# Quarter pieces in the levels of a triangular inverse, one block for both passes, and a reordered VectorE queue in a pooling + RWKV-7 layer

## The reference

```python
mod = silu(c) @ w_ada + b_ada;  shift, scale, gate = split(mod, 3)
u = rms_norm(x, norm_gain) * (1 + scale) + shift
proj = u @ w_in                                   # 1024 -> pool v|g, then r|k|v|w_down|a_down|gate
y_pool = multiscale_pool(proj[pool v]) * silu(proj[pool g])
# RWKV-7, per head of 64, state S of 64 x 64:
#   S_t = S_{t-1} diag(w_t) + (S_{t-1} a_t) b_t^T + v_t k_t^T ;  y_t = S_t r_t
y_rwkv = group_norm(y) * lnx_w + lnx_b + (sum r*k*r_k) * v, times silu(gate)
h = x + gate * (concat(y_pool, y_rwkv) @ w_out)
return rms_norm(h, final_gain)
```

## Time and profile before

| | us |
|---|---|
| median of 3 runs | 2912.44 |
| time of the profiled execution | 2913.32 |
| its span, first to last instruction | 2911.6 |
| PE busy | 2801.9 |
| DVE busy | 1560.3 |
| ACT busy | 1096.5 |
| POOL busy | 477.5 |

### The profile page before, as it was taken

One profiled execution on the slowest core, in us unless ns is written; L12 is line 12 of the kernel. 1 busy time (PEld: TensorE's weight loads), 2 busy tenths in 40 slices (PEclk: granted clock), 3 DMA queues, 4 the chain that ended last, 5 costly groups with the idle time before them and its releaser, 6 DMA issues.

```text
span 2911.6 us, 75522 instructions
## 1 busy us (share of the span) xinstructions
PE 2801.9 (96%) x30981; PEld 2327.5 (80%) x30981; DVE 1560.3 (54%) x3137; ACT 1096.5 (38%) x2531; POOL 477.5 (16%) x627
## 2 busy tenths in 40 slices
PE   7999999999799999999999999999999999999996
PEld 6777777777588888888888888888888888888884
DVE  2421121121366666666666666666666666666664
ACT  3333333232133333344433333344443343344442
POOL 3201101101111211111111211111111211111210
PEclk8999999999899999999999999999999999999997
DMA  8622322322100000010000000000000000001000
GB/s 340 238 74 99 115 87 93 108 99 67 66 9 23 24 23 23 24 38 24 28 26 23 23 24 23 23 31 31 24 30 24 23 24 23 24 26 35 23 16 23
DMA packets 68707, 153.09 MB, mean 53 GB/s; under 512 B 3977, under 2 KB 37342, under 8 KB 66398
## 3 DMA queue, kind: packets, MB, share of 16 engines
q1 hardware_dynamic: 63134, 130.08, 12.9%
q0 software_dynamic: 1680, 11.01, 0.9%
q10 hardware_dynamic: 3632, 7.87, 0.7%
HBM read 98.61 MB, written 50.33 MB: 51 GB/s over the span
## 4 chain that ended last, share of the span: by engine, by line
PE 52%; DVE 11%; ACT 6%; issue 5%; DVEq 0%; DMA 0%; ACTq 0%
PE bank L928 26%; PE bank L977 12%; PE bank L964 8%; PE bank L1096 2%; DVE SV L1455 2%; DVE LA L1480 1%; ACT sig L1167 1%; ACT sig L1166 1%; DVE mix L1371 1%; PE bank L938 1%; DVE t L1400 1%; ACT UV L1257 1%; DVE LA L1476 1%; DVE kk L1407 1%; DVE t L1408 1%
## 5 line engine op out<-in xcount | busy, mean ns | idle before, releaser
L928 PE MATMUL bank<-xT,w 128*128 128x128 f32 x8704 | 1106.6, 281 | 7.4 <-DMA xT<-xt_dram 7.4
L928 PEld LDWEIGHTS bank<-xT,w 128*128 128x128 f32 x8704 | 1011.9, 192 | 43.5 <-issue 8.5
L1199 ACT ACTIVATE XX<-bank 128x256 f32<-128x256 f32 x320 | 123.0, 384 | 910.3 <-PE bank L977 897.9
L347 PE MATMUL bank<-xT,w 128*128 128x256 f32 x2048 | 448.6, 381 | 4.8 <-ACT xT L467 4.8
L347 PEld LDWEIGHTS bank<-xT,w 128*128 128x128 f32 x2048 | 391.6, 191 | 65.4 <-issue 10.5
L1465 DVE TENSOR_TENSOR XV<-bank,level_mask 128x256 f32<-128x256 f32 x320 | 132.9, 423 | 327.4 <-PE bank L977 318.1
L964 PE MATMUL bank<-wo,Y 128*128 128x512 f32 x512 | 233.5, 600 | 4.6 <-DVE Y L1425 4.6
L379 PE MATMUL bank<-wo,yc 128*128 128x512 f32 x512 | 226.5, 596 | 4.5 <-DVE yc L698 4.5
L977 PEld LDWEIGHTS bank<-XX,AI 64*64 64x64 f32 x5120 | 163.6, 136 | 63.5 <-issue 52.0
L671 DVE TENSOR_SCALAR gate<-gate 128x1024 f32<-128x1024 f32 x16 | 11.1, 694 | 368.0 <-ACT gate L487 368.0
L977 PE MATMUL bank<-XX,AI 64*64 64x64 f32 x5120 | 185.8, 222 | 4.6 <-DVE XX L1498 4.6
(11 more groups left out here) (182 smaller groups left out, 3588.2 us busy)
## 6 DMA issues: line engine op xcount, KB each, us to landing
x_in<-in_x SPq DMA_DIRECT2D x16, 1024.0 KB, 7.5
xr<-in_x SPq DMA_DIRECT2D x32, 512.0 KB, 4.4
xt_dram<-xT SPq DMA_DIRECT2D x32, 512.0 KB, 8.6
h_dram<-xr SPq DMA_DIRECT2D x32, 512.0 KB, 2.6
xT<-xt_dram SPq DMA_DIRECT2D x32, 512.0 KB, 3.3
gate_row<-h_dram SPq DMA_DIRECT2D x32, 512.0 KB, 3.3
out<-gate_row SPq DMA_DIRECT2D x32, 512.0 KB, 2.6
w<-in_w_in POOLq DMA_DIRECT2D x8, 1088.0 KB, 11.0
```

Of the source, the lines that this page charges most:

```text
L347: last = nc.tensor.matmul(bank[t // 2][:, (t % 2) * T1:(t % 2 + 1) * T1], w1[:, k, t * P:(t + 1) * P], xT[:, k, :], start=(k == 0), stop=( ...
L928: last = nc.tensor.matmul(bank[b][:, q * P:(q + 1) * P], w2[:, k, (t0 + q) * P:(t0 + q + 1) * P], xT[par][:, k, :], start=(k == 0), stop=( ...
L1199: s(nc.scalar.activation(XX[j][:, k].rearrange(flat), bank[2 + j][:, 256 * k:256 * (k + 1)], ACT.Copy), xx_ready, hold=False)
```

## The change

1. `inverses` works in four pieces for each product of a level: chunk j and a, a pair of the four head pairs. Each piece has a PSUM bank of its own (2, 3, 5, 6), `lx` in its columns 0 to 127 and `xx` in 128 to 255, and its own waits and signals. VectorE's masks and ScalarE's copies are of 128x128 in place of 128x256 elements. The fill behind `xx` is moved in front of it (3 half slots in place of 2 and 1), `other` stands there too, and so `lx` of the next level follows `xx` directly. The last level keeps 2 and 1.
2. On VectorE `new_state(1)` is split. The sum stays. The multiplication with the decay moves behind the LA writes of the next block. `shift(n+1, 3)` moves ahead of `replaced_key`. TensorE no longer waits for the state at the block's start, but for the sum ahead of the Gram products and for the state ahead of `from_state(0)`.
3. Both passes are in one block. The prologue of pass 2 stands ahead of the last `project_out` pair on TensorE; VectorE does those residuals within its prologue; SP issues the first `xT` loads before it stores the last h. Tiles are ordered anew so that a tile of pass 2 overlaps one of pass 1 that is done, with waits for that on PE, POOL, ACT and DVE.

The diff, without the re-indentation and cut to its core:

```diff
             def inverses(fill, other):
-                def heads(o, lhsT, rhs):
-                    for p in range(NP):
+                def heads(o, lhsT, rhs, a):
+                    for p in (2 * a, 2 * a + 1):
                         for e in range(2):
                             h = half(e)
-                            last = nc.tensor.matmul(o[h, p * HD:(p + 1) * HD], lhsT[h, p], rhs(h, p), start=True, stop=True)
+                            c = (p - 2 * a) * HD
+                            last = nc.tensor.matmul(o[h, c:c + HD], lhsT(h, p), rhs(h, p), start=True, stop=True)
                 for i in range(LV):
-                    for j in range(NC):
+                    for j, a in PIECES:
                         if i:
-                            s.wait(xx_ready, NC * (i - 1) + j + 1)
+                            s.wait(xx_ready, piece(i - 1, j, a))
                         else:
                             s.wait(x1_ready, j + 1)
                         let_through(pe, pe_gate)
-                        heads(bank[5 + j][:, 0:256], AI[j], lambda h, p: XX[j][h, 0, p]).then_inc(lx_ps.sem, 1)
-                    fill(2)
-                    for j in range(NC):
-                        s.wait(xv_ready, NC * i + j + 1)
+                        heads(level_bank(j, a)[:, 0:128], lambda h, p: AI[j][h, p], lambda h, p: XX[j][h, 0, p], a)\
+                            .then_inc(lx_ps.sem, 1)
+                    fill(3 if i < LV - 1 else 2)
+                    if i in (2, 3):
+                        other(i - 2)
+                    for j, a in PIECES:
+                        s.wait(xv_ready, piece(i, j, a))
                         if i:
                             s.wait(xt_ready, NC * (i - 1) + j + 1)
                         let_through(pe, pe_gate)
...
-                    fill()
-                    if i in (2, 3):
-                        other(i - 2)
+                fill()
+                s.wait(xx_ready, piece(LV - 1, 1, 1))
...
             def take_inverse(i):
-                for j in range(NC):
-                    s.wait(xx_ps, NC * i + j + 1)
-                    s(nc.scalar.activation(XX[j][:, k].rearrange(flat), bank[2 + j][:, 256 * k:256 * (k + 1)], ACT.Copy),
+                for j, a in PIECES:
+                    s.wait(xx_ps, piece(i, j, a))
+                    s(nc.scalar.activation(XX[j][:, k, 2 * a:2 * a + 2].rearrange(flat), level_bank(j, a)[:, 128:256], ACT.Copy),
                       xx_ready, hold=False)
...
             def level(i):
-                if i:
-                    for j in range(NC):
-                        s.wait(xx_ready, NC * (i - 1) + j + 1)
+                for j in range(NC):
+                    if i:
+                        s.wait(xx_ready, piece(i - 1, j, 1))
                         s(nc.vector.transpose(XX[j][:, 1].rearrange(flat), XX[j][:, 0].rearrange(flat)), xt_ready, hold=False)
-                for j in range(NC):
-                    s.wait(lx_ps, NC * i + j + 1)
-                    s(nc.vector.tensor_tensor(XV[j][:, :, :], per_head(bank[5 + j][:, 0:256]), ...
+                    for a in range(2):
+                        s.wait(lx_ps, piece(i, j, a))
+                        s(nc.vector.tensor_tensor(XV[j][:, 2 * a:2 * a + 2, :], per_head(level_bank(j, a)[:, 0:128]), ...
...
             # TensorE, run(n)
-                pv.wait(s_ready, NC)              # ahead of bonus_sum
+                pv.wait(sum_ready, 1)             # ahead of the Gram products
+                pe.wait_ge(h_ready1.sem, h_ready1.at(N1 - 1, 4))   # first block, ahead of the BK transposes
+                pv.wait(carried_ready, 1)         # in from_state(0)
...
             # VectorE, run(n): behind the LA writes
+                if not first:
+                    new_state(NC - 1, pv, carried_ready)      # the two L1455 multiplications of block n-1
                 s(nc.vector.tensor_copy(dend[:, :, :].unsqueeze(3), chunks(sig[:, 0])[:, :, :, C - 1:C]), hold=False)
...
             # VectorE, end of run(n)
-                new_state(1)
+                state_sum(1)                                  # the two L1452 additions
                 if ahead:
-                    replaced_key()
                     shift(n + 1, 3)
+                    replaced_key()
...
             # between the passes
+            # SP: after the last step of pass 1
+                sp.wait_ge(xT_stored, 32 * N1)
+                sp.wait_ge(proj_ps.sem, proj_ps.at(N1 - 1, 4))
+                first_loads()
                 store(N1 - 1)
+            # TensorE: run(N1 - 1), then meanwhile()
+                pe.wait_ge(w2_loaded, 16 * (KT + 1))
+                pe.wait_ge(u_ready1.sem, u_ready1.at(N1 - 1, PT))
+                for m in range(len(SLOTS)):
+                    project(m, 0, 0, prologue=True)
+                pe.wait_ge(gate_ready1.sem, gate_ready1.at(N1 - 1, 2))
+                low_rank()
+                key_norm()
                 for j in range(2):
                     project_out(N1 - 1, j)
+            # VectorE: after mixed(N1 - 1)
+                shift(0, 0); tanh(); shift(0, 1); [wo2 *= gate_row]; shift(0, 2); key(); shift(0, 3); clamp(0); clamp(1)
+                first_residual(N1 - 1, 0)
                 decay_sum(); new_key(); replaced_key()
+                first_residual(N1 - 1, 1)
```

More of the change, by code:

```diff
@@ L1012, in from_state @@
                         for p in range(NP):
                             for e in range(2):
[L1014 to L1022 removed]
+                                o = j * 256 + p * HD
@@ new lines, in run @@
+                                last = nc.tensor.matmul(bank[5][half(1 - e), o:o + HD], mix[:, 8 + p, j * C:(j + 1) * C],
+                                                        center[:, half(e)], start=True, stop=True)
+                    last.then_inc(vt_ps.sem, 1)
+                    s.wait(kt_ready, 1)
+                    s.wait(bk_ready, 1)
+                    s.wait(rg_ready, 1)
+                    if first:
+                        pe.wait_ge(h_ready1.sem, h_ready1.at(N1 - 1, 4))
+                    else:
+                        pv.wait(rs_ready, 1)
@@ L1037, in state_and_output @@
+                    last.then_inc(bt_ps.sem, 1)
+                    s.wait(lhs_ready, 1)
+                    if not first:
+                        pv.wait(sum_ready, 1)
+                    for j in range(NC):
                         for p in range(NP):
                             for e in range(2):
-                                last = nc.tensor.matmul(bank[7][half(e), p * HD:(p + 1) * HD], BT[e][:, j, p], UV[e][:, p],
-                                                        start=True, stop=True)
@@ L1041, in state_and_output @@
-                        last.then_inc(s_ps.sem, 1)
-                        if j:
-                            s.wait(y_ready, j)
-                        for p in range(NP):
-                            for e in range(2):
-                                o = bank[6][half(e), p * HD:(p + 1) * HD]
-                                nc.tensor.matmul(o, UV[e][:, p], SM[j][e][:, p, 1], start=True, stop=False)
-                                last = nc.tensor.matmul(o, SV[e][:, p], LA[e][:, p, j, 1], start=False, stop=True)
@@ new lines, in run @@
+                                last = nc.tensor.matmul(bank[((2, 3), (4, 7))[j][e]][:, p * P:(p + 1) * P], BK[half(e), p, j].rearrange(flat),
+                                                        LA[e][half(e), p, j].rearrange(flat), start=True, stop=True)
+                                if p == NP - 1:
+                                    last.then_inc(gram_ps.sem, 1)
+                    fill(6)
+                    s.wait(bt_ready, 2)
+                    inverses(fill, (lambda h: None) if first else out_half)
@@ new lines, in run @@
+                    from_state(0, first)
+                    if ahead:
+                        low_rank()
+                    solve(0)
+                    fill(2)
+                    state_and_output(0, first)
+                    fill(2)
+                    if ahead:
+                        key_norm()
+                    from_state(1)
+                    fill(1)
+                    solve(1)
+                    fill(2)
+                    state_and_output(1)
+                    fill(len(SLOTS))
@@ new lines, in run @@
+                    if not first:
+                        group_scale(1 - par)
+                    level(0)
+                    if not first:
+                        group_gate()
+                    if ahead:
+                        shift(n + 1, 0)
+                    level(1)
+                    if ahead:
+                        tanh()
+                    level(2)
+                    s.wait(erg_ready, 1)
+                    s(nc.vector.tensor_scalar(rgate[:, :, :], rgate[:, :, :], LN_MAX, None, ALU.min), gclamp_ready)
@@ new lines, in run @@
+                    level(3)
+                    if not first:
```

(26 more changed lines are left out.)

1939 lines of the change are left out of this document (957 added, 982 removed).

## The result

The changed kernel takes 2815.86 us (median of 4 runs, 2815.16 to 2816.39) against 2912.61 for the kernel before, a ratio of 0.9667 with a 95% interval of 0.9653 to 0.9682. The forecast was 2845 us with a range of 2822 to 2876. The direction was right, and the gain of 97 us was over 40% larger than the 67.5 forecast, outside the range.

What follows compares the result with a forecast made beforehand. TensorE's queue was taken to bound the kernel. Gains of 24 us (levels), 30 (block's end) and 13.5 (between the passes) summed to 67.5 us off the median 2912.4: 2845 us, range 2822 to 2876.

Steps and rivals of the forecast that it cites:

- What bounds it: In the 31 intervals between blocks, TensorE's queue sets the end at 65.4 us each, at granted clock 1.00.
- The block's end: Moving the shift and state multiplication removes 1.12 us of waits less 0.15 a block: 30 us, bounds 10 and 35.
- new waits: At the block's end, 0.2 us taken by nearness to the sums, spread as 0.15 us a block.
- The levels: Moved fills in the inverse's levels gain net 0.78 us a block, 24 us in 31 blocks, bounds 0 to 40.
- round trips: Between small and full tiles on TensorE, 0.32 us each; four gone a block, 1.28 us.
- The 0.12 us charged to each handoff: From xx to the next lx, assumed cost of TensorE's doubled waits, 0.5 us a block; bounds 0 and 0.32 each.
- zero margin: At xx to next lx, the first copy lets lx start at 0.96 us, just when PE arrives.
- GpSimd: At the block's end, the shift passes beside GpSimd's BK unslowed and kk waits 0.2 us; otherwise kk loses 1.0.
- Between the passes: Lacing pass 2's prologue with the last out projection brings block 0's first level forward 13.5 us, bounds 9 and 16.
- The last block: It has no fill and changes by some 2 us either way.
- The rivals: Handoffs eat round trips 2869 us (0.14); VectorE bounds block's start 2865 (0.12); slower 2941 (0.05); no change 2912 (0.03).
- The emptying of PSUM: In the levels, the handoffs rival: split copies, each awaiting its signal, remove the 24 us, giving 2869 us; chance 0.14.

Runs made afterwards that it cites:

- no_order: Kernel after with VectorE's old order at the block's end and TensorE's old wait for the state ahead of bonus_sum: 2870.9 us, ratio 0.9852.
- late_state: Kernel after with the state multiplication back at the block's end behind replaced_key, the shift staying moved: 2842.3 us, ratio 0.9759.
- chunks: Kernel after with whole chunks as pieces, two per product, copies and masks of 128x256: 2849.1 us, ratio 0.9782.
- shift_between: Kernel after with shift 3 moved between the two halves of BK on VectorE: 2842.3 us, ratio 0.9759.
- hold_gone: shift_between with GpSimd's BK product of later blocks cut to 4 of 64 columns, leaving out computation: 2815.4 us, ratio 0.9664.
- lace_only: Kernel after with the old end order and old fill places; quarter pieces and lacing stay: 2904.2 us, ratio 0.9971.

## Why the prediction was wrong

The mechanisms were the right ones. Two terms of the sum were mis-sized, both the same way: the block's end and the handoffs in the levels.

- **What bounds it** was right: TensorE's queue, at a granted clock of 1.00 inside the loop both times.
- **The block's end: the step that failed.** I sized it by the idle times, 1.12 us a block, less 0.15 of new waits: 30 us. The steps gave 1.62 a block, 50 us, and the undo 51 by its intervals, 55 by its time. (Even the idle was misread: 1.7 of the 8.3 us for LA stood in block 0, ahead of the 31 intervals, so what was printed came to 1.07 a block.) The prediction had said that a busy PE can lose time in its steps, read the levels by starts, and then read the block's end by the idle times. A late signal cost 0.15 to 0.17 us in its own step beyond the idle shown and up to 0.10 in the next one (`no_order`, `late_state`), and 0.28 with none shown in `chunks`. The 0.17 is the stretch by which neighbouring groups of matmuls overlap when the signal is in time. The new waits did not come: LA ended 0.45 us before the Gram products began (1674.09 to 1674.54).
- **The levels.** Four round trips of 0.32 us: from the first lx to `from_state(0)` it was 33.08 us (1729.03 to 1762.11) and is 31.83 (1682.03 to 1713.86), so 1.25 against 1.28. The price was right. The 0.12 us charged to each handoff was wrong, with nothing measured behind it: 24 us forecast, 39 found. What I took for zero margin had 0.09 more, since the copy took 0.28 and not 0.37. The quarter pieces are needed all the same, as `chunks` shows at 0.28 a handoff.
- **GpSimd.** That the shift would pass beside GpSimd's product and the multiplication would not was right. I had not seen that this is nearly half of the reorder's worth, 0.73 of 1.66 us a block: an operation with two SBUF inputs behind the sums meets the hold (`shift_between`, `hold_gone`).
- **Between the passes.** 13.5 us forecast, 9.5 found in the two traces. PE started the projection at 740.93 in place of 737.3, and 2.9 of those 3.6 us are a first pass that ended 2.9 later in that execution (730.97). The stretch itself, from there to block 0's first level, went from 88.07 to 75.66 us, 12.4 less. The waits that I had counted as removed are in part still there: PE waits 3.3 us for `xr` and 2.0 for LA. The slow clock shrank with the idle time, from 0.66 over 25.4 us to 0.81 over 18.0.
- **The last block** gave 3.2 us where I had 2 either way. That is no gain of the change: the kernel after took 71.2 us there the second time, 2.6 more than the kernel before.
- **The rivals** fell. The emptying of PSUM did not become the bound: four copies of 128x128 took 0.98 us beside 0.98 of matmuls. The section "PSUM Bottleneck" of the Trainium skill's page "TensorEngine Tiling (Array Packing)", which I had weighed for one of them, says that it may; this trace does not show it, and copies twice as wide lost 33 us (`chunks`). VectorE was at 66% in the loop and in time at each place.

The terms against the traces: 50 + 39 - 4.3 + 9.5 + 3.2 = 97. The 4.3 are the first two intervals. In the kernel before they took 65.78 and 65.20 us, so they gained 1.5 us, and not twice the 2.87 of the levels and the block's end:

```profile
788.62:853.84 65.22, 58.97 (x862) 54.91 (x861) 41.43 (x94) 24.73 (x69) 14.31 (x16) 0.95 0.07 26
853.84:918.13 64.29, 63.10 (x877) 55.14 (x876) 41.36 (x101) 27.70 (x76) 11.57 (x13) 1.00 0.08 27
```

Part of that is the slow clock, 0.95 in the first one, and part two gaps of 1.0 and 1.2 us in the middle of `from_state`, with no wait behind them. What they are stays open.

## What to carry to other kernels

On a pipelined engine, price a wait by the step from start to start against the same step undisturbed, not by the idle time shown: here the idle times named 32 of 85 us, and in `chunks` the waits named 0.5 of 33. Before you compare two totals to a few microseconds, look for a stretch that no edit touches, and see how much it varies. Group work by the array's tile shape, since each round trip cost 0.31 us here, and cut what follows it into pieces just small enough that the first copy is back when the last piece leaves. Put VectorE's operations with a PSUM input beside GpSimd's products and those with two SBUF inputs elsewhere.

## What the runs showed of the hardware that was not expected

- A wait that made a step 0.28 us longer left no idle time in its row: 0.17 of it was overlap between two groups of matmuls that was gone, and the 0.11 of idle were too short to be printed (`chunks`).
- The last block, without fills, took 64.8 to 72.2 us in the traces, at granted clocks of 0.67 to 0.75, and the kernel after alone took 65.4 and 71.2.
- Twice the waits and signals on TensorE, eight pieces a level, cost next to nothing: xx to lx is 0.98 us against 0.96 of matmuls, and `lace_only`, which has the pieces and the old order, takes 65.76 us an interval against 65.72 before.
- A copy of 128x128 from PSUM took 0.28 us on ScalarE with no per-partition scale, and 0.37 with one (L1178); of 128x256 it took 0.38 (L1199).
